# Branch C's turned heads: the undilated group's second key block only for the queries that see it

## The reference, cut to what matters

```
for g, (win, dil) in enumerate(C_PATTERNS):      # (128, 1), (512, 4), (2048, 16)
    qc, kc = rope(norm(cq)), rope(norm(ck))
    o_g, lse_g = dilated_group(qc, kc, vc, win, dil)
wts = softmax(stack(lses))
o_c = einsum('gbsh,gbshd->bshd', wts, stack(outs))
```

## Time and profile before

| what | value |
|---|---|
| median of 3 runs | 1180.99 us (1180.57 to 1181.22) |
| the profiled execution | 1182.1 us, its span 1180.3 us |
| PE busy in the span | 1174.4 us |
| DVE, ACT busy in the span | 822.2 us, 698.0 us |

### The profile page before, as it was taken

How to read it: one execution, slowest core, us unless ns; L and a number is a source line. 1 busy time by engine, 2 the same in 40 slices (tenths; PEclk the granted TensorE clock), 3 DMA queues, 4 the chain that set the end, 5 groups by cost and what they waited for, 6 DMA issues and landing times.

```text
span 1180.3 us, 18491 instructions
## 1 busy us (share of the span) xinstructions
PE 1174.4 (100%) x6808; PEld 1007.7 (85%) x6808; DVE 822.2 (70%) x1319; ACT 698.0 (59%) x1114; POOL 139.9 (12%) x129
## 2 busy tenths in 40 slices
PE   9999999999999999999999999999999999999998
PEld 7888888888888899999888888888888888999897
DVE  6787989987766764454567788989876767555544
ACT  6667866655544474555476677666654445655453
POOL 6211422300000000000021123232000000000000
PEclk9999999999999999999999999999999999999999
DMA  8655446554576556565756554465545665665653
GB/s 280 197 157 157 127 140 197 160 171 129 163 211 203 182 174 190 186 190 186 205 153 200 145 155 126 140 192 168 161 139 165 179 198 177 179 194 182 194 182 105
DMA packets 127878, 204.75 MB, mean 173 GB/s; under 512 B 9206, under 2 KB 50736, under 8 KB 127792
## 3 DMA queue, kind: packets, MB, share of 16 engines
q1 hardware_dynamic: 122528, 194.64, 54.7%
q10 hardware_dynamic: 4720, 8.92, 2.5%
q0 software_dynamic: 544, 0.03, 0.0%
HBM read 200.41 MB, written 1.05 MB: 171 GB/s over the span
## 4 chain that ended last, share of the span: by engine, by line
PE 95%; DMA 2%; DVE 2%; ACT 1%; POOL 1%; issue 1%; ACTq 0%; POOLq 0%; DVEq 0%
PE ps_d L1524 23%; PE ps_d L1526 22%; PE ps_d L1525 22%; PE ps_b L1515 5%; PE ps_b L1517 5%; PE ps_b L1516 5%; PE ps_b L1579 4%; PE ps_b L1555 3%; PE ps_b L1613 3%; PE ps_b L1587 2%; DMA raw<-in_m_w_kv_dram 1%; DMA raw<-in_w_in_dram 1%; DVE w_lo L1230 1%; PE ps_d L1478 0%; POOL root L984 0%
## 5 line engine op out<-in xcount | busy, mean ns | idle before, releaser
L1230 DVE TENSOR_TENSOR w_lo<-raw,w_hi 128x1024 fp32r<-128x1024 f32 (+3 forms) x382 | 450.6, 1185 | 265.5 <-ACT w_hi L1043 264.2
L1043 ACT ACTIVATE w_hi<-raw 128x1024 fp32r<-128x1024 f32 (+3 forms) x382 | 391.8, 1027 | 371.1 <-PE ps_d L1526 282.1
L1524 PE MATMUL ps_d<-w_hi,h_hi 128*128 128x512 f32 (+3 forms) x704 | 279.5, 397 | 0.0
L1526 PE MATMUL ps_d<-w_hi,h_lo 128*128 128x512 f32 (+3 forms) x704 | 267.3, 380 | 0.0
L1525 PE MATMUL ps_d<-w_lo,h_hi 128*128 128x512 f32 (+3 forms) x704 | 266.9, 379 | 0.0
L1524 PE MATMUL ps_d<-w_hi,r_hi 128*128 128x512 f32 (+1 forms) x552 | 217.5, 394 | 0.0
L1526 PE MATMUL ps_d<-w_hi,r_lo 128*128 128x512 f32 (+1 forms) x552 | 214.1, 388 | 0.0
L1525 PE MATMUL ps_d<-w_lo,r_hi 128*128 128x512 f32 (+1 forms) x552 | 214.0, 388 | 0.0
L1526 PEld LDWEIGHTS ps_d<-w_hi,h_lo 128*128 128x128 f32 x704 | 132.3, 188 | 25.1
L1524 PEld LDWEIGHTS ps_d<-w_hi,h_hi 128*128 128x128 f32 x704 | 132.5, 188 | 24.8 <-issue 2.9
L1525 PEld LDWEIGHTS ps_d<-w_lo,h_hi 128*128 128x128 f32 x704 | 132.8, 189 | 20.5
(11 more groups left out here) (172 smaller groups left out, 1158.6 us busy)
## 6 DMA issues: line engine op xcount, KB each, us to landing
raw<-in_w_in_dram SPq DMA_DIRECT2D x150, 512.0 KB, 3.7
raw<-in_w_up_dram SPq DMA_DIRECT2D x64, 512.0 KB, 3.7
raw<-in_w_down_dram SPq DMA_DIRECT2D x64, 512.0 KB, 3.7
raw<-in_w_branch_dram SPq DMA_DIRECT2D x32, 512.0 KB, 3.8
raw<-in_m_w_kv_dram SPq DMA_DIRECT2D x16, 512.0 KB, 5.8
raw<-in_w_out_dram SPq DMA_DIRECT2D x16, 512.0 KB, 4.2
early<-in_b_gate_dram ACTq DMA_DIRECT2D x16, 256.0 KB, 4.2
raw<-in_w_in_dram SPq DMA_DIRECT2D x12, 256.0 KB, 3.5
```

The lines of the kernel that those rows point to most:

```text
L1043: nc.scalar.activation(unit_in(w_hi, hi_up, u), unit_in(raw, raw_up, u), ACT.Copy).then_inc(hi_split, 1)
L1230: nc.vector.tensor_tensor(unit_in(w_lo, lo_up, u), unit_in(raw, raw_up, u), unit_in(w_hi, hi_up, u).bitcast(F32), ALU.subtract).then_inc(l ...
L1524: nc.tensor.matmul(o, hi[:, a["c"], cut], wh, start=a["first"], stop=False)
L1526: last = nc.tensor.matmul(o, lo[:, a["c"], cut], wh, start=False, stop=a["last"])
```

## The change

The second key block of the undilated group holds positions 128 to 255. Query q of a `tt` stands at position 2q + tt, so the queries 0 to 63 stand ahead of every key of this block and their probabilities there are all zero. The change turns and multiplies this block for the queries 64 to 127 alone:

- the second of the four transposes of a head reads partitions 64 to 127 of `prob_c` against the corner `ident[64:128, 64:128]`, and writes 64 columns in place of 128;
- the four turned blocks stand packed in PSUM and in `probT_c`: columns 0 to 127, 128 to 191, 192 to 319, 320 to 447;
- `pcopy` copies 448 columns for C in place of 512;
- in `pv` the matmul of the second block has 64 moving columns and adds to the queries 64 to 127 alone;
- the planner's costs of C's `pturn`, `pcopy` and `pv` are those of 448 columns in place of 512.

The scores, the mask, the exponential and the normalisation keep all 512 columns. Branches A, B and M keep their shapes.

```
--- before.py
+++ after.py
@@ -31,6 +31,9 @@
 C_BLOCKS = TT + C_G - 1
+C_TURNED = {0: (0, 0, P), 1: (P, P // 2, P // 2), 2: (P + P // 2, 0, P), 3: (2 * P + P // 2, 0, P)}
+C_WIDE = 3 * P + P // 2
+assert C_BLOCKS == len(C_TURNED) and S == 2 * P
@@ -426,10 +429,11 @@
-            pt = item("pturn", "PE", 0.06 + 0.108 * blocks, [nm], st=st, m=blocks)
+            wide = C_WIDE if branch == "C" else blocks * P
+            pt = item("pturn", "PE", 0.06 + 0.108 * wide / P, [nm], st=st, m=blocks)
             pt.opens = 1
-            pc = item("pcopy", "ACT", act_cost(blocks * P), [pt, (free_at, 3.0) if free_at is not None and free_at.kind == "vmove" else free_at],
-                      chain="pcopy", of=pt, st=st, m=blocks, free=free_at)
+            pc = item("pcopy", "ACT", act_cost(wide), [pt, (free_at, 3.0) if free_at is not None and free_at.kind == "vmove" else free_at],
+                      chain="pcopy", of=pt, st=st, wide=wide, free=free_at)
@@ -440,7 +444,8 @@
-        cost = 0.109 * len(sts) * first["blocks"] + 0.25 if branch != "M" else 0.218 * first["blocks"]
+        wide = C_WIDE if branch == "C" else first["blocks"] * P
+        cost = 0.109 * len(sts) * wide / P + 0.25 if branch != "M" else 0.218 * first["blocks"]
@@ -905,6 +910,10 @@
+        def turned_block(st, k):
+            return C_TURNED[k] if st["branch"] == "C" else (k * P, 0, P)
@@ -1126,12 +1135,12 @@
-                    t, st, m = a["of"], a["st"], a["m"]
+                    t, st, wide = a["of"], a["st"], a["wide"]
...
-                    nc.scalar.activation(turned_prob_of(st)[:, 0:m * P], ps_b[:, b, 0:m * P], ACT.Copy).then_inc(bank_free[b], 1)
+                    nc.scalar.activation(turned_prob_of(st)[:, 0:wide], ps_b[:, b, 0:wide], ACT.Copy).then_inc(bank_free[b], 1)
@@ -1584,7 +1593,9 @@
                     for k in range(a["m"]):
-                        last = nc.tensor.transpose(ps_b[:, b, k * P:(k + 1) * P], prob_of(st)[:, k * P:(k + 1) * P], ident[:])
+                        at_col, q0, nq = turned_block(st, k)
+                        last = nc.tensor.transpose(ps_b[:, b, at_col:at_col + nq], prob_of(st)[q0:q0 + nq, k * P:(k + 1) * P],
+                                                   ident[q0:q0 + nq, q0:q0 + nq])
@@ -1610,8 +1621,9 @@
-                            last = nc.tensor.matmul(ps_b[r0:r0 + d, b, c:c + P], v[:, vh * d:(vh + 1) * d],
-                                                    turned_prob_of(st)[:, k * P:(k + 1) * P], start=k == 0, stop=k == blocks - 1)
+                            at_col, q0, nq = turned_block(st, k)
+                            last = nc.tensor.matmul(ps_b[r0:r0 + d, b, c + q0:c + q0 + nq], v[:, vh * d:(vh + 1) * d],
+                                                    turned_prob_of(st)[:, at_col:at_col + nq], start=k == 0, stop=k == blocks - 1)
```

## The result

| | before | after |
|---|---|---|
| median of 5 runs | 1181.06 us (1180.57 to 1181.38) | 1187.43 us (1187.03 to 1187.81) |
| the profiled execution, and its span | 1182.1 us, 1180.3 us | 1187.81 us, 1186.0 us |

The ratio is 1.0053, with a 95% interval of 1.0042 to 1.0064: the change that takes columns away from TensorE makes the kernel 0.53% slower.

A forecast was written before the change was run, and what follows sets the result against it. TensorE, busy 1174.4 of 1180.3 us, was taken as the bound. Turns at +7.8 us and `pv` at -1.6 summed to +6.2 us, giving a median of 1187.2 us, range 1183.2 to 1191.5.

The forecast's parts named there:

- TensorE's list sets the time: In C's stages, every ns in TensorE's list goes into the time; ScalarE counts only if TensorE waits for it.
- The border: Change of stationary shape on TensorE: 0.15 us, two per C head step; with narrowing, +0.245 each, +7.8 us in all.
- The narrow transpose: Second transpose of each C turn: 64 columns at half cost, 0.055 us less each, -1.8 us over 32 without borders.
- The narrow `pv`: Second block's multiplication in C: 0.10 us less for each of 16 `pv`, -1.6 us.
- The copy: ScalarE's copy of C's turned blocks: some 536 ns, 1.7 us less of ScalarE, costed at nothing.
- The order: Planner's placement under new costs: places may shift, 1 us allowed in either direction, nothing in the sum.
- No switch for a transpose: Rival for C's turns: narrow transpose makes no shape-change cost, only narrowing left, -3.4 us, 1177.6 us; 10%.
- The queue: Rival: TensorE's queue takes loads early, only one border costs 0.09 us; 1180.5 us; 6%.
- The granted clock: Rival in C's stages: more drains make the clock fall to 1.2 GHz, 1208 us; 3%.

The follow-up runs named there:

- e2: Changed kernel with full transposes as in e1, but turned blocks at their old columns and 512 columns copied: 1179.57 us, ratio 0.9986.
- e3: Changed kernel with each C head's narrow transpose made twice, one right behind the other: 1189.97 us, ratio 1.0073.
- e4: Changed kernel with the narrow transpose made twice, the third block's transpose between them: 1199.37 us, ratio 1.0151.
- e5: Changed kernel with narrow transposes moved within a head, to meet in paired turns or stand right behind scores, 24 borders less: 1184.17 us.
- e1: Changed kernel with four full transposes per C head, second block first, then partly overwritten; packing, 448-column copy, narrow `pv` and planner costs kept: 1179.28 us.
- e9: Changed kernel with the second block's `pv` over 128 moving columns again, the turn staying narrow: 1189.17 us, ratio 1.0066.
- e7: Kernel before with only the planner's new costs, so old instructions in the new order: 1181.82 us, ratio 1.0005.
- e8: Changed kernel with the planner's costs of before, so changed instructions in the old order: 1187.40 us, ratio 1.0053.
- e6: Second block's transpose reads partitions 0 to 95 (`96*128`), the others full; output not the reference's: 1179.29 us, ratio 0.9984.

## Why the prediction was right

1187.2 us were predicted and 1187.43 measured, and the terms of the sum hold one by one. That the two agree to 0.2 us is in part luck: the interval of the ratio is 1.3 us wide to either side. The trace gives 6.1 us for what the sum put at 6.2.

- **TensorE's list sets the time.** It did: no wait was added, and 5.7 us of difference lie in the stretch where C's heads are, as much as its turns and `pv` account for. e2 shows the reverse side, 1.7 us of ScalarE that cost nothing.
- **The border.** Predicted at 0.15 from one switch behind scores, and that a transpose makes it too, which no row showed. The turn came out at 0.68, where 0.69 was predicted. From one matmul's start to the next in the trace of after, the median of the 32 turns is 0.203 us from the first transpose to the narrow one, 0.203 from there to the third, and 0.166 to the fourth, against 0.109 for each in the turns of before that stand behind a chunk. That is 0.57 for three steps in place of 0.33, so 0.245 for each turn, and 7.8 us. Its parts: 0.203 - 0.109 = 0.094 ahead of the first instruction in the new shape; 0.166 - 0.109 = 0.057 for the load that nothing hides. e3 and e4 give 0.147 for a border by the medians, e5 0.14; the traces of e3 and e4 give 0.142.
- **The narrow transpose.** 0.055 was taken. It can be read where a narrow one does not come first in its shape, so that its load is hidden: its step to the full one behind it is 0.147 us behind the scores in e5 and 0.153 as the second of two in e3 and e5. Less the 0.094 of the border that leaves 0.053 and 0.059. By the median an added one costs 0.07 (e3).
- **The narrow `pv`.** 1.6 predicted, 1.7 measured twice (e1, e9). 0.92 us in place of 1.02 is the number the prediction named.
- **The copy.** 536 ns predicted, 537 measured, and hidden (e2).
- **The order.** Nothing was put in the sum. Both ways of changing it alone (e7, e8) lie within the 1 us allowed. e7's median is 0.8 above that of before, but its traced execution, which took just the median, is only 0.2 longer from the first to the last `pv`; the rest lies ahead of the first one, where executions differ by more than that.
- **The rivals.** No switch for a transpose would have given 1177.6, and fell with the first `64*128` record. The queue hid no load: at every border of after, the load starts 1 to 3 ns ahead of its matmul. The granted clock stayed at 1.00 in C's stages, though e4 has 214 borders.

What the change was meant to do is right: half of the second block, an eighth of a head's 512 columns, is turned and multiplied for queries whose probabilities there are all zero. The change takes 1.7 us out of `pv`, would take some 1.8 out of the turns, and pays 9.6 (64 borders of 0.15) for getting at the latter.

## What to carry to other kernels

On TensorE an instruction's neighbours are a part of its price: before cutting one in a stream of full ones to half its rows, compare the start-to-start times in the trace where the shape of the stationary operand changes with those where it doesn't. Here two borders (0.30 us) stood against half a transpose (0.055 us). Cut the moving columns, as `pv` does, which changes no shape; and where a narrow shape is needed, put all of it side by side or next to work that has it already (e5). If a thing can be packed by letting a full write be written over (e1), that is cheaper than a narrow write.

## What the runs showed of the hardware

- A border costs 0.094 us plus the first load in the new shape, bare: 0.057 for an fp32 transpose of 128 rows (0.166 against 0.109), about the same for one of 64 rows (0.203 less the 0.094 and some 0.053 for its columns), 0.05 for `128*64` (323 against 273 ns), and 0.11 for a 512-column float32r matmul's 128 columns (0.43 against 0.23 less the 0.09). The Trainium skill (TensorEngine Tiling (Array Packing), Key Properties) lets a change of mode drain TensorE, but not a change of tile within one; the runs agree: two tiles of one mode side by side, as the two heads in the scores and `pv`, start 0.007 us apart and have no border, and 64 rows make one where 66 and 96 do not (e6).
- The recorded duration of a matmul holds the second part of a border and not the first. The 32 narrow transposes of after are recorded at 272 ns on average, as long as a full one without a border, though they stream half the columns. Behind the scores in e5, where the narrow one makes no border, it is recorded at 215 ns, 57 less, which is the bare load again. The 0.094 us stand in no duration. The group of after and, in a window of e5, that one record:

```profile
L1597 PE MATMUL ps_b<-ident,early 64*128 64x64 f32 x32 | 8.7, 272 | 0.0
```

```profile
L1605 PE MATMUL ps_b<-ident,early x1: 215/215/215, 260.6 to 260.6; 64*128 64x64 f32 x1
```

- TensorE was "busy" for 1180.4 of 1186.0 us with 150 borders and 1174.4 of 1180.3 with 86. Borders look like work on the page; only start-to-start times, or idle time ahead of the weight loads, show them.
